# Attention probabilities transposed in 32x32 blocks by VectorE, and head pairs on every fourth gate chunk

## What is computed

```python
h = rms_norm(x, g_pre_mix)
(a_u, a_v, b_q, b_k, b_v, c_b, c_c, c_x,
 d_cq, d_ckv, d_kr, gate_logits) = split_columns(h @ w_in)
out_a = chunked_sgu(...)      # A
out_b = moba_attention(...)   # B: softmax(q k^T / 8, causal) v, 4 heads of 64
out_c = short_conv_mixer(...) # C
out_d = mla_attention(...)    # D: softmax(q k^T / sqrt(96), causal) v, 4 heads of 64
gates = sigmoid(gate_logits)  # 4 x 1024 columns
merged = sum_i gates[i] * (branches[i] @ w_branch[i])
x = x + rms_norm(merged @ w_out, g_post_mix)
y = square(relu(rms_norm(x, g_pre_mlp) @ w_mlp_in)) @ w_mlp_out
x = x + rms_norm(y, g_post_mlp)
```

## Time and profile before

| | |
|---|---|
| median of 3 runs (lowest to highest) | 791.03 us (790.62 to 791.67) |
| span of the profiled execution, first to last instruction | 788.9 us |
| median less span | 2.1 us |
| PE busy, share of the span | 781.6 us, 99% |
| DVE busy | 506.3 us, 64% |
| ACT busy | 407.6 us, 52% |
| POOL busy | 62.3 us, 8% |
| DMA, mean over the span | 185 GB/s |

### The profile page before, as it was taken

One profiled execution on the slowest core, in us unless ns is written; L12 is line 12 of the kernel. 1 busy time (PEld: TensorE's weight loads), 2 busy tenths in 40 slices (PEclk: granted clock), 3 DMA queues, 4 the chain that ended last, 5 costly groups with the idle time before them and its releaser, 6 DMA issues.

```text
span 788.9 us, 11019 instructions
## 1 busy us (share of the span) xinstructions
PE 781.6 (99%) x4053; PEld 659.3 (84%) x4053; DVE 506.3 (64%) x706; ACT 407.6 (52%) x631; POOL 62.3 (8%) x86
## 2 busy tenths in 40 slices
PE   9999999999999999999999999999999999999997
PEld 6898778888888888888889987878888888888885
DVE  5677655559777556555666876554788856565663
ACT  7566656443575445443546575554436745444441
POOL 1210000006110000000020100000333000000000
PEclk9999999999999999999999999999999999999999
DMA  9696555554466656567826855555654675656531
GB/s 310 187 304 190 160 161 157 176 202 133 149 198 216 209 178 190 191 188 220 275 66 199 281 162 160 158 163 187 186 157 140 200 225 185 187 185 207 179 119 53
DMA packets 88200, 145.86 MB, mean 185 GB/s; under 512 B 10316, under 2 KB 51556, under 8 KB 88164
## 3 DMA queue, kind: packets, MB, share of 16 engines
q1 hardware_dynamic: 88020, 145.24, 59.3%
q10 hardware_dynamic: 144, 0.13, 0.1%
HBM read 144.31 MB, written 1.05 MB: 184 GB/s over the span
## 4 chain that ended last, share of the span: by engine, by line
PE 99%; DVE 0%; POOL 0%; ACT 0%; POOLq 0%; issue 0%; DVEq 0%
PE banks L1352 24%; PE banks L1354 24%; PE banks L1353 24%; PE banks L1400 11%; PE banks L1401 5%; PE banks L1404 2%; PE banks L1585 1%; PE banks L1448 1%; PE banks L1466 1%; PE banks L1403 1%; PE banks L1364 1%; PE banks L1440 1%; PE banks L1410 1%; PE banks L1372 0%; PE banks L1438 0%; PE banks L1518 0%
## 5 line engine op out<-in xcount | busy, mean ns | idle before, releaser
L860 DVE TENSOR_TENSOR w_lo<-raw,w_hi 128x1024 fp32r<-128x1024 f32 (+1 forms) x256 | 306.3, 1225 | 123.8 <-ACT w_hi L529 123.4
L529 ACT CAST w_hi<-raw 128x1024 fp32r<-128x1024 f32 (+1 forms) x256 | 257.0, 1041 | 107.5 <-PE banks L1404 46.3
L1352 PE MATMUL banks<-w_hi,xT_both 128*128 128x512 f32 (+2 forms) x472 | 183.1, 388 | 0.0
L1354 PE MATMUL banks<-w_hi,xT_both 128*128 128x512 f32 (+2 forms) x472 | 178.6, 378 | 0.0
L1353 PE MATMUL banks<-w_lo,xT_both 128*128 128x512 f32 (+2 forms) x472 | 178.4, 378 | 0.0
L1400 PE MATMUL banks<-xT_both,w_hi 128*128 128x512 f32 x364 | 130.4, 398 | 0.0
L1352 PE MATMUL banks<-w_hi,brT_hi 128*128 128x512 f32 x320 | 125.4, 392 | 0.0
L1354 PE MATMUL banks<-w_hi,brT_lo 128*128 128x512 f32 x320 | 124.7, 390 | 0.0
L1353 PE MATMUL banks<-w_lo,brT_hi 128*128 128x512 f32 x320 | 124.7, 390 | 0.0
L1352 PEld LDWEIGHTS banks<-w_hi,xT_both 128*128 128x128 f32 x472 | 88.8, 188 | 18.6 <-issue 1.7
L1354 PEld LDWEIGHTS banks<-w_hi,xT_both 128*128 128x128 f32 x472 | 88.7, 188 | 16.4
(11 more groups left out here) (202 smaller groups left out, 757.0 us busy)
## 6 DMA issues: line engine op xcount, KB each, us to landing
raw<-in_w_in_dram SPq DMA_DIRECT2D x88, 512.0 KB, 4.6
raw<-in_w_mlp_in_dram SPq DMA_DIRECT2D x64, 512.0 KB, 4.7
raw<-in_w_mlp_out_dram SPq DMA_DIRECT2D x64, 512.0 KB, 4.3
raw<-in_w_branch_dram SPq DMA_DIRECT2D x16, 512.0 KB, 4.3
raw<-in_w_out_dram SPq DMA_DIRECT2D x16, 512.0 KB, 3.5
gate_th<-in_w_in_dram SPq DMA_DIRECT2D x8, 512.0 KB, 8.5
raw<-in_w_in_dram SPq DMA_DIRECT2D x8, 352.0 KB, 6.5
x<-in_x_dram SPq DMA_DIRECT2D x4, 256.0 KB, 4.2
```

Of the source, the lines that this page charges most:

```text
L529: nc.scalar.copy(w_hi[:, c % RING, h * n:(h + 1) * n], raw_of(q)[:, 0:n]).then_inc(hi_ready, 1)
L860: v.tensor_tensor(w_lo[:, c % RING, cut], raw_of(q)[:, 0:n], w_hi[:, c % RING, cut].bitcast(F32), ALU.subtract).then_inc(lo_ready, 1)
L1352: nc.tensor.matmul(dst, l_hi, r_hi, start=first, stop=False)
L1354: return nc.tensor.matmul(dst, l_lo, r_hi, start=False, stop=last)
```

## The change

- `head_transpose` and `head_copy` are gone. DVE transposes instead, in 16 instructions per pair of heads: each reads 32 partitions, 6 blocks of 32 columns (three 128-column blocks of two heads), and writes the transposed 32x32 blocks into 32 partitions of `probsT`.
- DVE inverts the row sums of a pair in one instruction; ACT, not DVE, scales `probs` (four instructions per pair).
- Scores of a pair stand after chunks 13, 17, 21 and 25. The values of the pair before stand in the same run after chunks 17, 21 and 25; those of the last pair stand after unit 3 of the branch products, in bank 2. The products of A stand after chunk 17. So PE leaves the large products for this work five times per layer instead of ten.
- With p's scores after chunk c, DVE does 5 of the 16 transposes after the split at step c + 2, 5 after that at step c + 3, and 6 ahead of that at step c + 4. For the last pair the steps end at 28: its last six stand three behind gating of unit 0 and three behind gating of unit 1.
- ACT and DVE split the output of branch D after unit 3, ahead of the split of chunk 32; unit 0 waits for branches A to C only, and units of branch D for D.

```diff
+        SCORES_AFTER = (13, 17, 21, 25)
+        VALUES_AFTER = (17, 21, 25)
+        LAST_VALUES_AFTER = 3
+        BLOCKS = [(a, b) for a in range(4) for b in range(4)]
...
-            def head_copy(l, h):
-                act.wait_ge(probsT_psum, nth(l, 8, h))
-                nc.scalar.copy(probsT[:, h % 2, :], psum[:, 2, 0:3 * P]).then_inc(probsT_copied, 1)
+            def pair_normalise(l, p):
+
+                act.wait_ge(inv_sum_ready, nth(l, 4, p))
+                for h in (2 * p, 2 * p + 1):
+                    for t in range(T):
+                        part = probs[:, h % 2, 0:P] if t == 0 else probs[:, h % 2, P:3 * P]
+                        last = nc.scalar.activation(part, part, ACT.Copy,
+                                                    scale=inv_sum[:, h // 4, t, h % 4:h % 4 + 1])
+                last.then_inc(probs_normed, 1)
...
+                if s - 1 in SCORES_AFTER:
+                    pair_exp(l, SCORES_AFTER.index(s - 1))
+                if s - 2 in SCORES_AFTER:
+                    pair_normalise(l, SCORES_AFTER.index(s - 2))
...
+                act.wait_ge(attn_psum, nth(l, 4, 3))
+                branch_hi(l, 3, psum[:, 2, :])
                 split(l, C_OUT)
...
+            def pair_transpose(l, p, blocks):
+
+                if blocks[0] == BLOCKS[0]:
+                    dve.wait_ge(probs_normed, nth(l, 4, p))
+                    if p >= 1:
+                        dve.wait_ge(attn_psum, nth(l, 4, p - 1))
+                flat = "p h (c n) -> p (h c) n"
+                for a, b in blocks:
+                    last = v.transpose(probsT[32 * b:32 * b + 32].rearrange(flat, n=P)[:, :, 32 * a:32 * a + 32],
+                                       probs[32 * a:32 * a + 32].rearrange(flat, n=P)[:, :, 32 * b:32 * b + 32])
+                if blocks[-1] == BLOCKS[-1]:
+                    last.then_inc(probsT_ready, 1)
...
+                if s - 4 in SCORES_AFTER:
+                    pair_transpose(l, SCORES_AFTER.index(s - 4), BLOCKS[10:])
...
+                    elif s - 2 in SCORES_AFTER:
+
+                        side_step(l, s)
+                        split(l, s + 3)
+                        pair_transpose(l, SCORES_AFTER.index(s - 2), BLOCKS[:5])
+                    elif s - 3 in SCORES_AFTER:
+
+                        side_step(l, s)
+                        split(l, s + 3)
+                        pair_transpose(l, SCORES_AFTER.index(s - 3), BLOCKS[5:10])
...
-                for n in range(4):
-                    gate_unit(l, n)
+                gate_unit(l, 0)
+                pair_transpose(l, 3, BLOCKS[10:13])
+                gate_unit(l, 1)
+                pair_transpose(l, 3, BLOCKS[13:])
+                gate_unit(l, 2)
+                gate_unit(l, 3)
+                branch_lo(l, 3, ORDER_D, psum[:, 2, :])
                 split_half(l, C_OUT, 0)
...
-            def head_transpose(l, h):
-                pe.wait_ge(probs_normed, nth(l, 16, 2 * h + 1))
...
             def pair_values(l, p):
 
-                pe.wait_ge(probsT_copied, nth(l, 8, 2 * p + 1))
+                pe.wait_ge(probsT_ready, nth(l, 4, p))
...
+                    if n == LAST_VALUES_AFTER:
+                        pair_values(l, 3)
```

More of the change, by code:

```diff
@@ L603, in merged_hi, with pair_exp @@
                                          ACT.Copy, scale=0.5).then_inc(mergedT_hi_ready, 1)
[L605 to L610, removed]
-            def head_copy(l, h):
-                act.wait_ge(probsT_psum, nth(l, 8, h))
-                nc.scalar.copy(probsT[:, h % 2, :], psum[:, 2, 0:3 * P]).then_inc(probsT_copied, 1)
+            def pair_exp(l, p):
+                for h in (2 * p, 2 * p + 1):
+                    for t in range(T):
+                        act.wait_ge(scores_masked, nth(l, 16, 2 * h + t))
+                        part = probs[:, h % 2, 0:P] if t == 0 else probs[:, h % 2, P:3 * P]
+                        nc.scalar.activation(part, part, ACT.Exp, bias=neg_max[:, h % 2, t:t + 1], scale=-1.0,
+                                             accum_out=row_sum[:, h // 4, t, h % 4:h % 4 + 1]).then_inc(probs_ready, 1)
+            def pair_normalise(l, p):
+                act.wait_ge(inv_sum_ready, nth(l, 4, p))
+                for h in (2 * p, 2 * p + 1):
+                    for t in range(T):
+                        part = probs[:, h % 2, 0:P] if t == 0 else probs[:, h % 2, P:3 * P]
+                        last = nc.scalar.activation(part, part, ACT.Copy,
+                                                    scale=inv_sum[:, h // 4, t, h % 4:h % 4 + 1])
+                last.then_inc(probs_normed, 1)
             def branch_hi(l, i, src):
@@ L965, in head_mask, with pair_inverse @@
                                        ALU.add, ALU.min, neg_max[:, h % 2, 1:2]).then_inc(scores_masked, 1)
[L967 to L976, removed]
+            def pair_inverse(l, p):
+                dve.wait_ge(probs_ready, nth(l, 16, 4 * p + 3))
+                n = 2 * (p % 2)
+                v.reciprocal(inv_sum[:, p // 2, :, n:n + 2], row_sum[:, p // 2, :, n:n + 2]
+                             ).then_inc(inv_sum_ready, 1)
+            def pair_transpose(l, p, blocks):
[9 more added lines that the diff above has]
+                    last.then_inc(probsT_ready, 1)
             def branch_lo(l, i, order, src):
@@ L1084, in side_step @@
                     branch_lo(l, 2, ORDER_C, conv.rearrange("p f n -> p (f n)"))
[L1085 to L1088, removed]
+                if s - 1 in SCORES_AFTER:
+                    p = SCORES_AFTER.index(s - 1)
+                    if (l, p) != (0, 0):
+                        dve.wait_ge(probsT_ready, nth(l, 4, p - 1))
+                    head_mask(l, 2 * p)
+                    head_mask(l, 2 * p + 1)
+                if s - 2 in SCORES_AFTER:
+                    pair_inverse(l, SCORES_AFTER.index(s - 2))
+                if s - 4 in SCORES_AFTER:
+                    pair_transpose(l, SCORES_AFTER.index(s - 4), BLOCKS[10:])
+                if s == 18:
                     dve.wait_ge(sv_psum, nth(l, 1, 0))
@@ L1096, in side_step @@
                     v.scalar_tensor_tensor(a_out, u2, 0.5, a_out, ALU.mult, ALU.mult).then_inc(a_out_ready, 1)
-                if s == 16:
+                if s == 19:
                     branch_lo(l, 0, ORDER_A, a_out)
-                if s in (19, 23):
-                    n = (s - 19) // 4
-                    branch_lo(l, (1, 3)[n], (ORDER_B, ORDER_D)[n], psum[:, (3, 5)[n], :])
+                if s - 1 == VALUES_AFTER[1]:
+                    branch_lo(l, 1, ORDER_B, psum[:, 3, :])
             def gate_unit(l, n):
@@ L1441, in pair_scores @@
                                      ).then_inc(scores_psum, 1)
-            def head_transpose(l, h):
-                pe.wait_ge(probs_normed, nth(l, 16, 2 * h + 1))
[L1445 to L1450, removed]
             def pair_values(l, p):
-                pe.wait_ge(probsT_copied, nth(l, 8, 2 * p + 1))
+                pe.wait_ge(probsT_ready, nth(l, 4, p))
                 if p == 0:
                     pe.wait_ge(u_gelu, nth(l, 1, 0))
-                if p == 2:
-                    pe.wait_ge(ropeT_copied, nth(l, 2, 1))
                 f = p % 2
-                bank = psum[:, (3, 5)[p // 2], f * S:(f + 1) * S]
+                bank = psum[:, (3, 2)[p // 2], f * S:(f + 1) * S]
                 for t in range(T):
@@ L1533, in side_after @@
                     last.then_inc(ropeT_psum, 1)
-                if c == 14:
+                if c in SCORES_AFTER:
+                    pair_scores(l, SCORES_AFTER.index(c))
+                if c == 17:
                     pe.wait_ge(ln_ready, nth(l, 1, 0))
@@ L1544, in side_after @@
                     last.then_inc(sv_psum, 1)
[L1545 to L1550, removed]
+                if c in VALUES_AFTER:
+                    pair_values(l, VALUES_AFTER.index(c))
             def gain_columns():
@@ L1658, in _ @@
                     if n == 0:
+                        pe.wait_ge(brT_lo_ready, nth(l, 4, ORDER_B))
+                    if i == NB - 1:
                         pe.wait_ge(brT_lo_ready, nth(l, 4, ORDER_D))
```

16 lines of the change are left out of this document (5 added, 11 removed).

## The result

| | before | changed |
|---|---|---|
| median of 5 runs (lowest to highest) | 790.99 us (790.62 to 791.67) | 798.04 us (797.31 to 798.36) |
| span of the profiled execution | 788.9 us | 796.2 us |
| mean granted TensorE clock | 0.999 | 0.991 |

The account below looks back on a forecast made before the run. PE was taken as the bound, busy 781.6 of 788.9 us. 2 x (3.0 wait - 2.9 saved) = +0.2 us gave a span of 789.1; medians lie 2.1 above, so 791.2, written 791.3, range 788.4 to 795.5.

Parts of the forecast that it names:

- What PE saves: PE's side work of attention and branch A falls by 2.9 us per layer (2.2 to 3.5), 5.8 us in two.
- four joins: Scores with branch A's products, those with values, and twice scores with values: 0.4 us saved per layer, between 0 and 0.8.
- Pairs 0 to 2 hidden: DVE's transposes for the first three pairs end about 3 us early, so PE doesn't wait at chunks 17, 21 or 25.
- t: Time of one DVE transpose from start to start, taken as 0.28 us, with bounds of 0.21 and 0.47.
- the two-input rows: DVE instructions of 128 and 32 elements: 1.04 ns per element plus 0.07 us fixed, so 0.27 us for 192 elements.
- The estimate by the Trainium skill: For a DVE transpose: 378 ns duration, about 0.29 us from start to start, and a sum of 791.7 us.
- the formula: Change's worth by transpose time t: 2 x (11 t - 2.95) - 0.1 us, from eleven transposes ahead of the last values.
- G: Start of unit 0, 169.47 in the trace before; the last values were to start at G + 8.5, a 3.0 us wait per layer.
- the row above speaks against it: Argument against the clock rival: at the span's end PE has nothing for 4.5 us and the clock still shows 1.00.
- The clock: Rival: clock falls in the wait ahead of the last values, 2 us lost per layer, 795.3 us; chance 0.09.
- the two rivals on the slower side: Dearer DVE transposes (chance 0.18) and the clock falling in the wait (chance 0.09).
- a dearer transpose: Rival, eleven transposes between chunk 31 and last values: 793.4 us at t 0.38, 795.3 at 0.47; chance 0.18.

Follow-up runs that it names:

- part-alone experiment: Kernel before, plus only eleven unused DVE transposes behind the split of chunk 31 and PE's wait for the last of them after unit 3: 803.77 us, ratio 1.0163.
- best version: Changed kernel with every pair one gate chunk earlier, ACT's second tanh ahead of the exponentials and rotated-key copies moved to step 14: 786.02 us, ratio 0.9939.
- with 8 transposes: Changed kernel with three of the last pair's 16 transposes left out, so 8 remain behind chunk 31 and part of the values is wrong: 794.79 us, ratio 1.0053.
- version one chunk earlier: Changed kernel with scores, values and branch A's products one chunk earlier and no transposes among the gatings: 788.13 us, ratio 0.9966.

## Why the prediction was wrong

**What PE saves: right.** 2.9 us per layer were forecast, 2.5 for transposes and 0.4 for four joins. The runs sum to 3.04; the part-alone experiment leaves 5.7 for two layers. How the joins share it was not as thought. A joined run, behind chunk 17:

```profile
104.03 0.39 PE L1395 MATMUL banks<-w_hi,xT_both 128*128 128x512 f32 x1
104.35 0.49 PE L1479 MATMUL banks<-kTB,qTB 64*128 64x128 f32 x4
104.67 0.60 PE L1481 MATMUL banks<-kTB,qTB 64*128 64x256 f32 x4
105.20 1.14 PE L1574 MATMUL banks<-gate_th,av 128*64 128x128 f32 x16
106.13 0.87 PE L1496 MATMUL banks<-probsT,proj 128*64 128x256 f32 x8
106.93 0.50 PE L1393 MATMUL banks<-w_hi,xT_both 128*128 128x512 f32 x1
107.26 0.40 PE L1394 MATMUL banks<-w_lo,xT_both 128*128 128x512 f32 x1
```

107.26 - 104.03 - 0.454 = 2.78 us. Its parts apart come to about 3.3 (scores 1.05, values 1.0, branch A about 1.3 once the transposes beside it are taken off): 0.5 saved by two joins. The two joins of D's scores with values save nothing (2.31 against about 1.3 + 1.0).

**Pairs 0 to 2 hidden: right.** DVE's eleven transposes of pair 0 end at 101.74, 4.4 us ahead of the values in the fence above (forecast: 3).

```profile
97.53 4.21 DVE L993 STREAM_TRANSPOSE probsT<-probs 32x192 f32<-32x192 f32 x11
```

**The step that failed first: t.** The sum took "0.28, by the two-input rows". Measured is 0.384 from start to start, inside the bounds of 0.21 and 0.47 and somewhat above their middle. The fixed 0.07 us came out near (0.06, from two widths); the element costs 1.7 ns from start to start, not 1.04. The estimate by the Trainium skill, "VectorE: DVE Perf Modes", "The three transpose paths", came to 378 ns of duration, and the trace has 369: its duration agrees. The overlap that turned this into 0.29 from start to start does not (and by the formula 0.29 makes 791.5; the 791.7 belong to 0.30). DVE's next transpose starts 0.015 us behind the end of the one ahead, while two-input instructions overlap by 0.08. With t = 0.384 the formula gives G + 9.55; the gating steps, 0.72 and not 0.60 us between transposes, and a first transpose that starts at G + 4.17 and not G + 4.04, do the rest to G + 9.86. Together this makes 3.0 us into 4.3 and 791.3 into 793.9.

**The step that cost most: "the row above speaks against it".** The clock had a chance of 0.09, because at the end of the program PE rests for 4.5 us at 1.00. But the clock fell in both layers of three kernels, for waits of 3.2 and 4.3 us. One row of a rest that happened to keep its clock was taken as a rule. The traces that came later have the same rest behind PE's last matmul, and it doesn't always keep its clock for so long: in the changed kernel, whose last matmul ends at 790.47, the clock falls after 2.2 us.

```profile
790.50:792.70 2.20, 0.00 (x0) 0.00 (x0) 1.33 (x3) 0.69 (x2) 0.74 (x2) 1.00 0.00 0
792.70:796.10 3.40, 0.00 (x0) 0.00 (x0) 1.03 (x3) 0.00 (x0) 0.00 (x0) 0.50 0.44 154
```

It falls after 2.3 us in the best version, after 2.8 with 8 transposes, and after 3.8 to 4.8 in the other traces. The 4.8 are the kernel before: that row was the longest of all, and a rest of 3.0 us lies in the range where the clock may fall. The rival's own price, 2 us per layer, was right: 4.1 us here for both. The rule of the Trainium skill, "TensorE: Matmul & The Clock Gate", "HAM oscillation", that idle gaps between bursts send the clock back to half, is what these traces show for gaps from 3.2 us, and not for those up to 1.7. What was also missed is that the two rivals on the slower side are one chain: a dearer transpose lengthens the wait, and the longer wait brings the clock down. The prediction priced them apart, at 793.4 and 795.3, and nowhere their sum; 0.2 + 2.6 for the longer waits + 4.1 for the clock + 0.6 for the start, on 790.99, gives 798.5; measured 798.04.

**Not settled.** The first scores start 0.4 to 1.1 us later in the changed kernel and its variants with the same order than in the kernel before and in the part-alone run (80.61 in both). No changed instruction stands ahead of them; no run tells the cause. The delay lies within the first 17 us of the program: the changed kernel's first large product starts at 8.05 us, before at 7.47. The version one chunk earlier has it too, and the best version doesn't, in one trace each, so about 0.5 us of the step between these two may be this and not the moves on ACT.

## What to carry to other kernels

Work that is moved from the bounding engine to one that is idle by a third pays only where its deadline leaves room: three quarters of it were hidden here, and the last quarter, with eleven instructions between a split that can't come earlier and a product that waits, gave back twice what the move saved. Price such a wait together with the clock: here the waits of 0.6 and 1.7 us cost their own length, and each of those of 3.2 and 4.3 us cost another 1.5 to 2.8 us at half clock. When an order is written out by hand, move the whole chain one place earlier before giving up on it, and then look at what its first link pushes back on the other engines (here a tanh, 2 us of waits). And don't rest a low chance on one row: the same rest at the end of the program kept its clock for 4.8 us in one trace and for 2.2 in another.

## What was not expected of the hardware

- A transpose on DVE of 32 partitions x 192 float32 elements takes 369 ns and one of 96 elements 248 ns. At 192 elements it doesn't overlap with the transpose ahead of it, at 96 it does by 0.03 us, so from start to start an element costs about 1.7 ns. Plain two-input instructions need 1.04.
- The low clock lasted 3.4 or 6.8 us, each for the same wait in another layer or kernel, and began in the wait (174.88 in one that starts near 171.8), at its end, or a microsecond behind it. How long it lasts decides between 1.5 and 2.8 us and could not be told beforehand from the wait's length. At the end of the program, with no matmul left, the clock fell after 2.2 to 4.8 us.
- Filling a wait with 38 small products kept the clock at 1.00, and the values behind them started no later (G + 9.85, without them G + 9.86).
